# A two-block layer kernel: triangle inversion with masks at the eviction, two row norms folded into one scale, and later weight loads

## The reference, cut to what matters

```python
def first_block(...):
    ...
    x = x + peer(rmsnorm(x, norm_ffn_g), peer_wq, peer_subkeys, peer_u, peer_v)
    return rmsnorm(x, final_norm_g)
def second_block(x, ...):
    h = _rmsnorm(x, norm1)
    proj = h @ w_in            # 40 blocks of 256 columns in the kernel, and 16 gate columns
    o_a = _gated_delta_rule(...)
    o_b = _hgrn2_recurrence(...)
    ...
```

```python
    a_kk = jnp.einsum('nbhid,nbhjd->nbhij', kb, kc) * decay
    lhs = jnp.eye(CHUNK) + jnp.tril(a_kk, -1)
    sol = lax.linalg.triangular_solve(lhs, rhs, left_side=True, lower=True, unit_diagonal=True)
```

## Time and profile before

| | |
|---|---|
| median of 3 runs | 2077.7 us (2076.5 to 2079.97) |
| the profiled execution | 2080.77 us, of it 2078.6 us span |
| PE busy | 1730.2 us (83%) |
| DVE busy | 1340.5 us (64%) |
| ACT busy | 924.7 us (44%) |
| POOL busy | 859.3 us (41%) |
| DMA | 637.15 MB, mean 307 GB/s |

### The profile page before, as it was taken

One profiled execution on the slowest core, in us unless ns is written; L12 is line 12 of the kernel. 1 busy time (PEld: TensorE's weight loads), 2 busy tenths in 40 slices (PEclk: granted clock), 3 DMA queues, 4 the chain that ended last, 5 costly groups with the idle time before them and its releaser, 6 DMA issues.

```text
span 2078.6 us, 22827 instructions
## 1 busy us (share of the span) xinstructions
PE 1730.2 (83%) x7686; PEld 1069.4 (51%) x7686; DVE 1340.5 (64%) x2906; ACT 924.7 (44%) x2363; POOL 859.3 (41%) x778
## 2 busy tenths in 40 slices
PE   8987988877877777887889898887889878777786
PEld 7985444322322222787889898884444322222222
DVE  4668667766766654598535675348677667667654
ACT  5554554444444443544124334454544444444443
POOL 3335333333333332576355436544333333333331
PEclk9999999999999999999999999999999999999999
DMA  6447999999999999343013233448999999999996
GB/s 227 136 158 307 421 420 420 421 422 421 421 422 421 421 421 385 98 137 112 21 41 102 82 102 122 151 165 360 420 421 421 422 421 421 422 421 422 421 422 290
DMA packets 102052, 637.15 MB, mean 307 GB/s; under 512 B 11264, under 2 KB 12544, under 8 KB 36272
## 3 DMA queue, kind: packets, MB, share of 16 engines
q0 software_dynamic: 75216, 543.27, 62.9%
q1 hardware_dynamic: 26720, 92.43, 13.9%
HBM read 634.61 MB, written 1.05 MB: 306 GB/s over the span
## 4 chain that ended last, share of the span: by engine, by line
PE 38%; DMA 37%; DVE 13%; ACT 7%; issue 3%; POOL 1%; SPq 0%; DVEq 0%; ACTq 0%; POOLq 0%
DMA arena<-in_uv,arena 30%; PE pb L587 15%; DMA spare<-in_uv,arena 6%; PE pb L336 5%; PE pb L337 4%; PE pb L338 4%; DVE arena L1555 3%; ACT arena L1004 3%; PE pb L409 1%; PE pb L700 1%; POOL parts L1991 1%; PE pb L714 1%; PE pb L709 1%; PE pb L792 1%; ACT arena L999 1%
## 5 line engine op out<-in xcount | busy, mean ns | idle before, releaser
L587 PE MATMUL pb<-arena 128*128 128x512 f32 x1848 | 916.5, 626 | 224.9 <-ACT arena L1004 223.9
L1555 DVE SCALAR_TENSOR_TENSOR arena<-arena,pb 128x1024 f32<-128x1024 f32 x462 | 563.4, 1220 | 372.7 <-DMA arena<-in_uv,arena 372.6
L2013 POOL DMA_INDIRECT arena<-in_uv,arena x462 | 440.3, 953 | 721.2 <-PE pb L587 701.1
L587 PEld LDWEIGHTS pb<-arena 128*128 128x128 f32 x1848 | 325.2, 193 | 782.0 <-ACT arena L1004 515.2
L1991 POOL TENSOR_TENSOR parts<-ring,parts 128x512 fp32r<-128x512 f32 x228 | 335.0, 1485 | 360.2 <-ACT parts L847 339.0
L996 ACT ACTIVATE arena<-arena 128x1 f32<-128x1 f32 x512 | 103.2, 202 | 616.4 <-DVE arena L1555 556.8
L847 ACT ACTIVATE parts<-ring 128x512 fp32r<-128x512 f32 x328 | 201.5, 627 | 255.6 <-PE pb L338 252.8
L336 PE MATMUL pb<-xl,parts 128*128 128x256 f32 x704 | 223.6, 318 | 9.3 <-DVE xl L1249 5.9
L1004 ACT ACTIVATE arena<-cst,arena 128x128 f32<-128x128 f32 x512 | 205.5, 401 | 47.2 <-ACT arena L999 0.4
L336 PE MATMUL pb<-parts,xh 128*128 128x256 f32 x608 | 179.9, 296 | 28.1 <-POOL parts L1991 17.6
L337 PE MATMUL pb<-xh,parts 128*128 128x256 f32 x704 | 202.4, 287 | 0.0
(11 more groups left out here) (287 smaller groups left out, 1810.3 us busy)
## 6 DMA issues: line engine op xcount, KB each, us to landing
ring<-in_w_in SPq DMA_DIRECT2D x108, 512.0 KB, 3.5
ring<-in_wq SPq DMA_DIRECT2D x32, 512.0 KB, 4.4
ring<-in_w_out SPq DMA_DIRECT2D x16, 512.0 KB, 4.0
arena<-in_uv,arena POOLq DMA_INDIRECT x462, 20.2
ring<-in_wa SPq DMA_DIRECT2D x8, 512.0 KB, 3.6
ring<-in_wb SPq DMA_DIRECT2D x8, 512.0 KB, 3.5
arena<-in_sk POOLq DMA_DIRECT2D x2, 1024.0 KB, 6.2
arena<-in_tail POOLq DMA_DIRECT2D x1, 1280.0 KB, 9.6
```

The costliest lines, as they stand in the source:

```text
L587: ins = pe.matmul(ys[hf][:, :], diags[:, k % 4, :], lands[k % LANDS][:, D + hf * 512:D + (hf + 1) * 512], start=k % (8 * K) == 0, stop=k % ...
L1555: ve.scalar_tensor_tensor(z, z, 1.0, xg[t], ALU.mult, ALU.mult, accum_out=hidden[:, k:k + 1]).then_inc(*up("v_dot", ("dot", e, k)))
L2013: gp.indirect_dma_start(lands[k % LANDS], None, rows_uv, bass.IndirectOffsetOnAxis(ap=eidx[:, k:k + 1], axis=0)).then_inc(*up(f"dma_rows{k ...
```

## The change

Nothing is left out of the computation. Three parts change.

1. The two norms between the blocks. With gain row w and sum of squares s, the final norm followed by the first norm of the next block is one scale of `z = x * w`. DVE multiplies by the gain in place (`row_squares`), sums the squares of that as well, and both inverse roots come from one square root (`row_root`) and one reciprocal (`row_scaled`). The second is put on the diagonal of a 128 x 128 matrix, and PE multiplies `z` with it in place of the transposes (`scaled_features`). The high and low halves are written per token tile (`scaled_hi`, `scaled_lo`), and tile 0's are done during the experts of tile 1.
2. The weights of mixer 2 are not loaded or split during the experts. SP waits for the last gather to have landed before the first block of `w_in2`, and `cap` stops ACT, DVE and POOL there (`mixer2`) until the experts are over.
3. The inversion. `LT` keeps all levels and gets ones on its diagonal. A step is: PE makes `LT`ᵀ`X` whole; DVE takes it out of PSUM times a matrix of signs (`signs[lev]`, 7 new constants, which adds 448 KB to the load at L1995); PE multiplies this with only the odd columns of `XT` (64 of 128); DVE copies the odd columns in; PE transposes `XT`, and ACT copies the even columns into `X`. POOL has no part in it. `ET` and its masks, `dX`, and the two subtractions are gone.

```diff
+    for lev in range(NLEV):
+        mask = parts[4 + lev]
+        parts.append(np.eye(P) - (mask.T if lev else mask))
...
+        mixer2 = first_piece["w_in2"]
...
-            def normed(tag):
-                pq.wait_ge(*on((tag, "scaled", 1)))
-                features((tag), lambda t, c: work[:, t * D + c * P:t * D + (c + 1) * P])
...
+                    if e == 1 and k == 8 * K + 14:
+                        scaled_features(0)
+            def scaled_features(t):
+                pq.wait_ge(*on(("row_diag", t)))
+                for c2 in range(4):
+                    o = bank(("n1", t, c2), None if t else 4 + c2)
+                    for c in range(2):
+                        ch = 2 * c2 + c
+                        ins = pe.matmul(o[:, c * P:(c + 1) * P], xA[:, t, ch * P:(ch + 1) * P], row_diag[:, t, :],
+                                        start=True, stop=True)
+                    ins.then_inc(*full(("n1", t, c2)))
...
-            normed("n1")
+            scaled_features(1)
...
+            def inverse_turned(lev, g):
+                o = bank(("X", lev, g))
+                pq.wait_ge(*on(("XT", lev, g)))
+                for s in range(4):
+                    ins = pe.transpose(o[:, s * P:(s + 1) * P], XT[:, g, s, :], ident)
+                ins.then_inc(*full(("X", lev, g)))
...
-                o = bank(("E0", g))
-                pq.wait_ge(*on(("E", 0, g)))
-                for s in range(4):
-                    ins = pe.transpose(o[:, s * P:(s + 1) * P], ET[:, g, s, :], ident)
-                ins.then_inc(*full(("E0", g)))
+                inverse_turned(0, g)
...
             def inverse_y(lev, g):
                 o = bank(("Y", lev, g))
-                pq.wait_ge(*on(("E", lev, g)))
-                pq.wait_ge(*on(("X", lev - 1, g)))
+                pq.wait_ge(*on(("M", g)))
+                pq.wait_ge(*on(("taken", ("X", lev - 1, g))))
                 for s in range(4):
-                    ins = pe.matmul(o[:, s * P:(s + 1) * P], ET[:, g, s, :], X[:, g, s, :], start=True, stop=True)
+                    ins = pe.matmul(o[:, s * P:(s + 1) * P], LT[:, g, s, :], X[:, g, s, :], start=True, stop=True)
                 ins.then_inc(*full(("Y", lev, g)))
...
+            def inverse_xt(lev, g):
+                o = bank(("XT", lev, g))
                 pq.wait_ge(*on(("taken", ("Y", lev, g))))
...
+                m = 2 ** lev
                 for s in range(4):
...
+                    z = XT[:, g, s, :].rearrange("p (n two m) -> p n two m", two=2, m=m)[:, :, 1, :]
+                    ins = pe.matmul(o[:, s * 64:(s + 1) * 64], Y[:, g, s, :], z, start=True, stop=True)
+                ins.then_inc(*full(("XT", lev, g)))
...
+            for n, (lev, g) in enumerate(steps):
+                if (4 * lev + g) % 8 == 7:
+                    item()
+                inverse_y(lev, g)
+                if n >= 1:
+                    inverse_xt(*steps[n - 1])
+                if n >= 2 and steps[n - 2][0] < NLEV - 1:
+                    inverse_turned(*steps[n - 2])
+            inverse_xt(*steps[-1])
...
-            pos, cut, cap = [0], [0], [behind_wa]
+            pos, cut, cap = [0], [0], [mixer2]
...
-            stats("n1")
-            features_hi("n1", lambda c: gains["n1"][:, c:c + 1], ("full", ("wq", 7)))
+            cap[0] = behind_wa
+            pos[0] -= PARTS
+            for c in range(0, 8, 2):
+                ahead(1)
+                scaled_hi(1, c)
+                scaled_hi(1, c + 1)
...
-                    copy(Y[:, g], bank4(key), key)
+                    copy(even(X[:, g], 2 ** lev), even(bank4(key), 2 ** lev), key)
...
+            def row_squares(t):
+                vq.wait_ge(*on(("final_by", 1)))
+                for hf in range(2):
+                    xs = xA[:, t, hf * 512:(hf + 1) * 512]
+                    vq.wait_ge(*on(("fin_squares", 1, t, hf)))
+                    vq.wait_ge(*on(("taken", ("y", 1, t, hf))))
+                    ve.tensor_tensor(xs, xs, final_by[:, hf * 512:(hf + 1) * 512], ALU.mult).then_inc(
+                        *up("v_norm", ("row_z", t, hf)))
+                for hf in range(2):
+                    xs = xA[:, t, hf * 512:(hf + 1) * 512]
+                    vq.wait_ge(*on(("row_z", t, hf)))
+                    ve.scalar_tensor_tensor(pb[place["y", 1, t, hf]][:, :], xs, 1.0, xs, ALU.mult, ALU.mult,
+                                            accum_out=row_ss[:, t, hf:hf + 1]).then_inc(*up("v_norm", ("row_ss", t, hf)))
...
+            def row_scaled(t):
+                vq.wait_ge(*on(("row_root", t)))
+                ve.reciprocal(row_r[:, t, :], row_r[:, t, :]).then_inc(*up("v_norm", ("row_rs", t)))
+                vq.wait_ge(*on(("row_rs", t)))
+                ve.tensor_scalar(row_diag[:, t, :], ident, row_r[:, t, 1:2], None, ALU.mult).then_inc(
+                    *up("v_scaled", ("row_diag", t)))
...
+            def row_final(t):
+                vq.wait_ge(*full(("n1", t, 3)))
+                ve.tensor_scalar(xA[:, t, :], xA[:, t, :], row_r[:, t, 0:1], None, ALU.mult).then_inc(
+                    *up("v_final", ("final", 1, t)))
...
-                ve.tensor_tensor(ET[:, g], LT[:, g], bm(masks[0], 4), ALU.mult).then_inc(*up("v_inverse", ("E", 0, g)))
-                vq.wait_ge(*on(("E", 0, g)))
-                ve.tensor_tensor(XT[:, g], bm(ident, 4), ET[:, g], ALU.subtract).then_inc(*up("v_inverse", ("XT", 0, g)))
-                vq.wait_ge(*full(("E0", g)))
-                ve.tensor_tensor(X[:, g], bm(ident, 4), bank4(("E0", g)), ALU.subtract).then_inc(*taken(("E0", g)))
...
+                ve.copy_predicated(LT[:, g], bm(ident.bitcast(U32), 4), bm(ones, 4)).then_inc(*up("v_inverse", ("M", g)))
+                vq.wait_ge(*on(("M", g)))
+                ve.tensor_tensor(XT[:, g], LT[:, g], bm(signs[0], 4), ALU.mult).then_inc(*up("v_inverse", ("XT", 0, g)))
...
+            def inverse_y(lev, g):
+                key = ("Y", lev, g)
                 vq.wait_ge(*full(key))
...
+                ve.tensor_tensor(Y[:, g], bank4(key), bm(signs[lev], 4), ALU.mult).then_inc(*taken(key))
...
+                ve.tensor_copy(odd(XT[:, g], m), pb[place[key]][:, 0:256].rearrange("p (s n m) -> p s n m", s=4, m=m)).then_inc(
+                    *taken(key))
...
-                gq.wait_ge(*on(("dot", e, NT * 8 * K - 2)))
-                ahead(PARTS)
...
-            for lev in range(1, NLEV):
-                for g in range(4):
-                    if (4 * lev + g) % 8 == 7:
-                        item()
-                    key = (("E0", g) if lev == 1 else ("Y", lev - 1, g))
-                    gq.wait_ge(*on(("full", key)))
-                    gq.wait_ge(*on(("XT", 0, g)))
-                    gp.tensor_tensor(ET[:, g], LT[:, g], bm(masks[lev], 4), ALU.mult).then_inc(*up("g_inverse", ("E", lev, g)))
+            for _ in range(3):
+                item()
...
+                if (name, i) == ("w_in2", 0):
+                    sq.wait_ge(*on(("rows", 1, NT * 8 * K - 1)))
                 sp.dma_start(ring_of(k), d[name][i]).then_inc(*up(f"w_slot{k % SLOTS}", None, 16))
```

More of the change, by code:

```diff
@@ L125, in build @@
         masks = [cst[:, (4 + k) * P:(5 + k) * P] for k in range(NLEV)]
+        signs = [cst[:, (4 + NLEV + k) * P:(5 + NLEV + k) * P] for k in range(NLEV)]
         gains = {"mix": cols[:, 0:8], "ffn1": cols[:, 8:16], "n1": cols[:, 16:24], "ffn2": cols[:, 24:32]}
@@ L204, in build, with odd, even @@
         btv, kdv, eGv = v2(sv["beta"]), v2(sv["kd"]), v2(sv["eG"])
-        LT, X, XT, ET, Y = (region(o, 2048, g=4).rearrange("p g (s n) -> p g s n", s=4)
-                            for o in (6144, 8192, 24576, 26624, 28672))
+        LT, X, XT, Y = (region(o, 2048, g=4).rearrange("p g (s n) -> p g s n", s=4)
+                        for o in (6144, 8192, 24576, 28672))
+        def odd(ap, m):
+            return ap.rearrange("p s (n two m) -> p s n two m", two=2, m=m)[:, :, :, 1, :]
+        def even(ap, m):
+            return ap.rearrange("p s (n two m) -> p s n two m", two=2, m=m)[:, :, :, 0, :]
         AQ = region(30720, 2048, g=4).rearrange("p g (s n) -> p g s n", s=4)
@@ new lines, in inverse_xt @@
+                ins.then_inc(*full(("XT", lev, g)))
+            steps = [(lev, g) for lev in range(1, NLEV) for g in range(4)]
+            for n, (lev, g) in enumerate(steps):
[7 more added lines that the diff above has]
+            inverse_xt(*steps[-1])
@@ L868, in root @@
                 ac.activation(dst, dst, ACT.Sqrt).then_inc(*up("a_root", (tag, "root")))
-            def stats(tag):
-                for t in range(NT):
-                    aq.wait_ge(*on((tag, "x", t)))
-                    ac.activation(work[:, t * D:(t + 1) * D], xA[:, t, :], ACT.Square,
-                                  accum_out=small[:, t:t + 1]).then_inc(*up("a_squares", (tag, "squares", t)))
-                root(small[:, 0:NT], tag)
             def squares(tag, i, ready):
@@ L1102, in scalar_program @@
```

(31 more changed lines are left out.)

141 lines of the change are left out of this document (83 added, 58 removed).

## The result

The changed kernel took 2061.07 us, the median of 4 runs (2059.79 to 2063.35), against 2078.84 us of the kernel before in the same job (4 runs, 2076.5 to 2082.68): ratio 0.9912, interval 0.9900 to 0.9924. It is 0.9% faster: 10.0 us behind the forecast of 2051.1, and 2 us inside the upper end of the range of 2042 to 2063. The span fell by 19.0 us, from 2078.6 to 2059.6, where the sum had 26.6; that is 7.6 of the 10.0. The rest is that the forecast set the median 3.1 us under the profiled execution, as it was before the change, and here it lies 0.3 under it (2061.39), less 0.4 by which the time around the span is shorter.

What follows compares the result with a forecast made beforehand. Bounds by stage: DMA bytes in the experts, a chain between blocks, PE's queue and waits in the inversion. 5.0 + 3.3 + 18.9 - 0.6 = 26.6 us off 2080.8 gives 2054.2, median 3.1 lower: 2051.1, range 2042 to 2063.

Steps and rivals of the forecast that it cites:

- Later weight loads: Experts: moving four blocks of mixer 2's weights behind the last gather saves 5.0 us of DMA (bounds 0 and 5.0).
- the cover that I gave it: Experts: tile 0's added work lies under the gathers; a 3 to 4 us delay empties the 20.2 us queue by a fifth.
- The chain: Between the blocks: PE starts 1.9 us earlier, the mixer's first block is full at 851.0; gain 3.3 us (bounds 0 and 5.1).
- the fourth piece's 1.44 us of products: Between the blocks: the mixer's first block needs the fourth split piece, at 849.5, and 1.44 us of products: full at 851.0.
- The head: Start of the inversion: one more DVE operation before the transposes costs 0.78 us a group, +3.1 us (bounds 2.8 and 5.3).
- The steps: Inversion: from 93.6 to 71.6 us, 22.0 saved (bounds 15.3, POOL's pauses and their clock alone, and 23.5).
- The 1.5 us for features ahead of signs: Inversion steps: PE may wait where DVE finishes an item's features before the next signs, 0.5 us for each of three.
- Held steps: Rival, inversion: new waits or the clock hold the step at 2.68 us; 8 us less gain, 2059; chance 0.16.
- First parts nothing: Rival: the first two parts, later loads and chain, give nothing; 8.3 us less gain, 2059.4; chance 0.10.
- Columns: Rival, inversion: streaming half the columns does save, 192 records at 0.055 instead of 0.110; 10.6 more, 2040.5; chance 0.05.
- Lockstep: Rival, inversion: PE's order exposes the hops, 4.6 us a step; 30 us slower, 2107; chance 0.04.
- The start: Load at the start: 448 KB more of constants cost 0.6 us (bounds 0 and 1.1).

Runs made afterwards that it cites:

- early loads: The changed kernel without SyncE's wait for the last gather, so four blocks of mixer 2's weights load among the gathers: 2064.02 us, ratio 0.9920.
- all columns: The changed kernel with all 128 columns of `XT` streamed instead of the 64 odd ones: 2059.58 us, ratio 0.9908.
- inversion alone: The kernel before with only the new inversion, its norms and weight loads as before: 2065.31 us, ratio 0.9925.
- POOL's order: The kernel before with POOL's three weight splits of the inversion put three steps later in its queue, behind those steps' masks: 2067.11 us, ratio 0.9942.
- products ahead: The changed kernel with the next group's products put ahead of this group's transposes in the head: 2050.13 us, ratio 0.9849.
- exponential moved: The kernel with the next group's products ahead of transposes, plus ACT's exponential and six small DVE operations moved earlier: 2047.27 us, ratio 0.9852.
- filled pauses: The changed kernel with nine thrown-away identity products ahead of each of PE's four waits for signs in the head: 2056.73 us, ratio 0.9892.

## Why the prediction was right, and by what it was off

The mechanism of each part held but for the clock in the head, and the sum was 7.6 us too large. That the result still falls into the range is partly luck. The forecast had its own range, 2045 to 2057, and 2061.07 lies outside it, nearer to the two rivals at 2059 and 2059.4, which are what the upper part of the whole range was there for. One of the signs that the prediction named for being wrong, a fall of the clock in the head, came.

**Later weight loads.** Forecast 5.0, and 5.3 by removing the wait alone. The dots run ahead in steps of 1.25 us, one for each block of 512 KB. By choice 72 they are 5.1 us ahead of the kernel before. Two pauses of about 0.95 us at choices 203 and 247, which the kernel before doesn't have, follow. The first is made up by choice 216; the second comes too close to the end, and 4.3 us are left at the last dot. All seven traces with the new norms have these pauses, also the one with the loads back among the gathers, and the three with the old norms have none; which part of the change brings them was not tried. At choice 136 the dots are 2.2 us late beside the added work of tile 0, and by 139 they have made that up, so the cover that I gave it was there.

**The chain.** Forecast 3.3, measured 2.4 (15.8 to 13.4 us). Two terms were off in opposite directions. PE started earlier than I had it, 4.0 us behind the addition instead of 4.45. But the step that set the end was not the fourth piece's 1.44 us of products: pieces were not the pace. PE's first products run without a gap from 843.08 for 5.8 us, to 848.9, and DVE does L1709, L1723 and L1725 back to back until 849.12, with no wait behind them; in this trace the two ends are too close to say which set it. The sum had left PE's products out: its own end of the features, 846.9, and four pieces of 1.44 us behind it are 852.7, not 851.0, a gain of 1.6 us. That the gain came out larger is due to the features, done 7.3 us behind the addition instead of 8.2. Before the change DVE had the latter two done 3.5 us ahead of its wait's end, in 0.21 and 0.29 us; here they take 1.31 and 1.28, beside POOL's splits. I had "full at 851.0", 12.3 us behind the addition; DVE took it up at 13.4. The size of the gain also hangs on the clock. Over the ten traces this way is 15.8 to 16.8 us with the old norms and 13.4 to 14.6 with the new, 16.4 and 14.0 in the mean. In each kind it is 0.7 to 1.3 us longer where the low clock beside it lasts 3.4 us longer. In four of the seven with the new norms DVE waits 0.7 to 3.3 us for PE's products there, so PE sets the end.

**The head.** Forecast +3.1, measured +6.5: this is the step that failed. Its work was sized rightly, 4.6 us a group with a pause of "about 2.1 us", and I named the clock as a risk in a rival and left it out of the sum, on "pauses of 1.4 leave the clock at 1.00". Pauses of 2.15 us in 4.59 didn't. Filling them returned 3.5 us of the head. The other traces with the same order of PE's real work in the head bear it out, without dummy products: the head is 20.1, 21.0, 22.0 and 24.1 us at a mean clock of 0.92 (early loads), 0.82 (all columns), 0.73 (changed kernel) and 0.61 (inversion alone), against 18.5 at 1.00. The lower level goes on into the steps until 1010 and costs some 4.2 us there, which is 72.5 less 67.8 of work and the wait of 0.46 (8 records of `XT` take 1.94 us at 1005.90 instead of 1.00). Together nearly 8 us in this execution, as much as the whole miss; the other errors nearly cancel.

**The steps.** Forecast -22.0, measured -21.1, but as two errors against each other. The work was smaller than I had it: 2.17 us a step and not 2.27, since 64 columns take 0.84 and transposes 0.44; 24 x 1.73, 20 x 0.44 and 17.5 for items are 67.8 us where I had 70.1. The 1.5 us for features ahead of signs didn't come: the changed kernel has one wait of PE for signs in all steps, 0.46 us. It stands behind DVE's wait of 3.1 us for the exponential, an instruction I had not read in DVE's queue, and it is gone where the exponential was moved. The clock's 4.2 us took the place of both. POOL's order was the larger part, as the forecast had it (its lower bound of 15.3 was these pauses and their clock alone; 13.6 measured).

**The rivals.** Held steps: not in the steady state, where covers held; its clock came in the head. First parts nothing: refuted by 5.3 and 2.4. Columns: refuted, 0.05 us a step. Lockstep: refuted, no step is above 2.2 us at full clock.

**The start.** 0.6 forecast, +1.4 seen, inside the scatter of 5.8 us of that stage: neither shown nor refuted. The same goes for the 1.0 us lost behind the first `U`: that rest is 984.3 to 986.7 us over the ten traces, and 986.7 is that of the kernel with POOL's order, whose program there is the one before.

## What to carry to other kernels

When an operation is added to a chain between two of PE's groups, price the pause that PE gets twice: its length, and what the granted clock does behind it. Here the second was nearly 8 us against 6.5 - 3.5 = 3.0. It is not a fixed price: the other traces with this head have head and steps at 90.5 to 96.6 us, the changed kernel's at 94.5. Look next for work already in PE's queue that can stand in front of the wait: reordering gave back more than dummy products, and an item of real products put there gave most. And read the whole queue of the engine that feeds a new wait, down to operations of one column for another part of the kernel, and the queue of the engine that these wait for in turn.

## What was not expected of the hardware

Dummy products pay. 72 records that compute nothing made the head 3.5 us shorter, and the granted clock, 1.00 instead of 0.73, is what differs (for the whole kernel 0.9892 against 0.9912, intervals that overlap). In the changed kernel two pauses of 2.15 us, 4.59 us apart, came ahead of a fall to 1.2 GHz. One was enough elsewhere: a single long pause of 1.93 us (products ahead), 1.94 (exponential moved) or 2.08 (filled pauses) ended 0.2 to 1.6 us ahead of a fall. Pauses of 1.38 us every 3.83 us didn't bring one in the kernel before, nor in the same head of the kernel with POOL's order (clock 1.00 in both).

Once fallen, the clock stayed low for 20 us in the changed kernel and 27 in the one with the inversion alone, with more pauses in the head meanwhile. It was low for 3.4 us behind the single pauses of 1.94 and 2.08 us, and for 10 where a pause of 1.27 followed the fall. The same head of PE's queue met the fall early in the kernel with the inversion alone, in the third group in the changed one, and later still in the one with the early loads; what sets the moment was not tried.

On DVE, a cast and a subtraction of 128 x 128 that take 0.21 and 0.29 us took 1.31 and 1.28 us beside POOL's splits of 1.3 us. It is not a matter of the change: in four of the ten traces (changed kernel, products ahead, all columns, early loads) each of the two starts within 0.6 us behind the start of a split and takes 1.27 to 1.41 us; in the six others no split has begun ahead of them, and they take 0.21 to 0.22 and 0.29. A predicated copy of whole runs took 0.72 us in the head, as an ordinary operation of that size does.
